# Token-major rows in the experts' feature order, and the memory's value units within the cross-attention

## The reference

```python
def memory_cross_attention(x, mem, w_q, w_kv, w_o):
    q = (x @ w_q).reshape(B, S, H, E)                  # 4 heads of 256
    kv = (mem @ w_kv).reshape(B, M, 2, H, E)
    s = jnp.einsum('bshe,bmhe->bhsm', q, kv[:, :, 0]) * (E ** -0.5)
    p = jax.nn.softmax(s, axis=-1)
    o = jnp.einsum('bhsm,bmhe->bshe', p, kv[:, :, 1])
    return o.reshape(B, S, D) @ w_o

def hier_moe(h, ...):      # top group of 4, top 2 of its 8 experts, per token
    for e in range(N_EXPERTS):
        hid = jax.nn.silu(xf @ w_gate[e]) * (xf @ w_up[e])
        y = y + combine[:, e:e + 1] * (hid @ w_down[e])
```

## Time and profile before

| | |
|---|---|
| median of 3 runs | 2835.76 us |
| the profiled execution | 2834.82 us |
| its span | 2833.0 us |
| mean granted clock | 0.972 |
| DVE busy | 1257.0 us (44%) |
| ACT busy | 1204.8 us (43%) |
| POOL busy | 981.4 us (35%) |
| HBM read | 307.22 MB |

### The profile page before, as it was taken

One profiled execution on the slowest core, in us unless ns is written; L12 is line 12 of the kernel. 1 busy time (PEld: TensorE's weight loads), 2 busy tenths in 40 slices (PEclk: granted clock), 3 DMA queues, 4 the chain that ended last, 5 costly groups with the idle time before them and its releaser, 6 DMA issues.

```text
span 2833.0 us, 36207 instructions
## 1 busy us (share of the span) xinstructions
PE 2687.5 (95%) x13862; PEld 2164.5 (76%) x13862; DVE 1257.0 (44%) x2335; ACT 1204.8 (43%) x1762; POOL 981.4 (35%) x437
## 2 busy tenths in 40 slices
PE   7998999899998999999979998999989999989998
PEld 5774886688886888888858866888858877768886
DVE  3555505443234122223256154532358336257997
ACT  3555523423234243434335324232353355346775
POOL 3221542345453333233305423444432335431000
PEclk9999999999999999999999999999998999999999
DMA  4111331233324322222113312333213422239997
GB/s 154 60 45 45 119 119 34 71 104 89 104 78 153 90 75 72 63 75 63 58 60 118 106 45 71 93 98 95 84 55 103 149 75 75 60 106 330 397 397 290
DMA packets 321050, 317.24 MB, mean 112 GB/s; under 512 B 16490, under 2 KB 278011, under 8 KB 320420
## 3 DMA queue, kind: packets, MB, share of 16 engines
q1 hardware_dynamic: 318596, 307.26, 33.4%
q0 software_dynamic: 2288, 7.88, 0.7%
q10 hardware_dynamic: 16, 0.03, 0.0%
HBM read 307.22 MB, written 19.48 MB: 115 GB/s over the span
## 4 chain that ended last, share of the span: by engine, by line
issue 48%; PE 27%; POOL 16%; DVE 3%; DMA 3%; ACT 1%; SPq 1%; POOLq 0%; ACTq 0%; DVEq 0%
POOL wl L692 12%; PE ps L2021 8%; PE ps L2022 8%; PE ps L2023 8%; POOL wl L689 4%; DMA e_raw<-in_w_up 3%; DVE e_wl L1808 2%; PE ps L2017 1%; SPq L630 1%; PE ps L2567 1%; PE ps L2332 1%; ACT e_wh L1310 0%; PE ps L2410 0%; PE ps L2429 0%; PE ps L2400 0%
## 5 line engine op out<-in xcount | busy, mean ns | idle before, releaser
L689 POOL TENSOR_TENSOR wl<-raw,wh 128x1024 fp32r<-128x1024 f32 (+1 forms) x191 | 453.1, 2372 | 1566.6 <-ACT wh L756 1566.4
L2021 PE MATMUL ps<-xh,wh 128*128 128x512 f32 x1680 | 680.9, 405 | 58.3 <-issue 29.7
L2022 PE MATMUL ps<-xh,wl 128*128 128x512 f32 x1680 | 665.6, 396 | 0.0
L2023 PE MATMUL ps<-xl,wh 128*128 128x512 f32 x1680 | 665.4, 396 | 0.0
L692 POOL TENSOR_TENSOR wl<-raw,wh 128x1024 fp32r<-128x1024 f32 (+1 forms) x191 | 478.4, 2505 | 0.0
L756 ACT ACTIVATE wh<-raw 128x1024 fp32r<-128x1024 f32 (+1 forms) x191 | 198.7, 1040 | 584.0 <-PE ps L2023 573.2
L2021 PEld LDWEIGHTS ps<-xh,wh 128*128 128x128 f32 x1680 | 322.3, 192 | 152.9 <-issue 60.3
L2023 PEld LDWEIGHTS ps<-xl,wh 128*128 128x128 f32 x1680 | 321.8, 192 | 70.4
L2022 PEld LDWEIGHTS ps<-xh,wl 128*128 128x128 f32 x1680 | 322.8, 192 | 63.5
L2021 PE MATMUL ps<-ah,wh 128*128 128x512 f32 x608 | 239.6, 394 | 5.4 <-DVE X L1534 2.4
L2023 PE MATMUL ps<-al,wh 128*128 128x512 f32 x608 | 236.7, 389 | 0.0
(11 more groups left out here) (367 smaller groups left out, 4082.3 us busy)
## 6 DMA issues: line engine op xcount, KB each, us to landing
raw<-in_ffn_w_in SPq DMA_DIRECT2D x88, 512.0 KB
raw<-in_dil_w_qkv SPq DMA_DIRECT2D x72, 512.0 KB
e_raw<-in_w_gate SPq DMA_DIRECT2D x56, 512.0 KB, 11.7
e_raw<-in_w_up SPq DMA_DIRECT2D x56, 512.0 KB, 12.9
e_raw<-in_w_down SPq DMA_DIRECT2D x56, 512.0 KB, 11.5
raw<-in_w_in SPq DMA_DIRECT2D x42, 512.0 KB
raw<-in_xatt_w_kv SPq DMA_DIRECT2D x32, 512.0 KB
raw<-in_ffn_w_out SPq DMA_DIRECT2D x32, 512.0 KB
```

The costliest lines, as they stand in the source:

```text
L689: pool.tensor_tensor(wl[:, s, 0:4, 0:n], raw[:, s, 0:4, 0:n], wh[:, s, 0:4, 0:n].bitcast(F32), ALU.subtract)
L2021: pe.matmul(dst, stat_h, mov_h, start=first, stop=False)
L2022: pe.matmul(dst, stat_l, mov_h, start=False, stop=False)
L2023: return pe.matmul(dst, stat_h, mov_l, start=False, stop=last)
```

## The change

It has two parts.

1. The four value units get numbers of their own (U_MV) behind the query units, on every engine. In the softmax stage they are placed by hand between scores and transposes. On ScalarE `values_out` waits for a value unit and makes the high part of the unit after next; VectorE's copies of the values (`cross_values`) stand between maxima and scalings. The transposes of tiles 0, 1 and 3 go to banks 2 and 3, those of tile 2 to 0 and 1. `x_q` moves to the place of `ah`, since the memory's high and low parts must last longer, and `x_e` has four buffers in place of two.
2. The step of 8 moves from TensorE's reads to ScalarE's copy into `e_tok`: it reads PSUM with the step and writes contiguously. Everything behind (`sorted_x`, `e_rows`, the product for tile 0, the transposes of later tiles) reads contiguously.

```diff
-        x_q = at("x_q", A0, [P, KC, T])
+        x_q = at("x_q", 114, [P, KC, T])
-        x_e = at("x_e", A0 + 16, [P, 2, 4 * M])
+        x_e = [at(f"x_e{n}", kb, [P, 4 * M]) for n, kb in enumerate((A0, A0 + 4, 106, 110))]
...
-        U_MQ = (24, 114)
+        U_MQ = (20, 110)
+        U_MV = (24, 114)
...
+        X_BANKS = (2, 2, 0, 2)
...
-                over(sp, U_MEM[layer], 8, lambda u, k: square(u, kv, (k * UC).v))
+                over(sp, U_MEM[layer], 4, lambda u, k: square(u, kv, (k * UC).v))
                 over(sp, U_MQ[layer], 4, lambda u, k: square(u, a["xatt_w_q"][layer], (k * UC).v))
+                over(sp, U_MV[layer], 4, lambda u, k: square(u, kv, (k * UC + D).v))
...
+                def cross_copy(i):
+                    act.wait_ge(x_tr, TT * layer + i + 1)
+                    act.activation(x_pt[:, :, i * P:(i + 1) * P],
+                                   flat[:, T * X_BANKS[i]:T * X_BANKS[i] + 1024].rearrange("p (k q) -> p k q", k=8), ACT.Copy
+                                   ).then_inc(x_ptr, 1)
+
+                def values_out(k):
+                    done(Lin(U_MV[layer] + k), 1)
+                    high(Lin(U_MV[layer] + k + 2))
+
+                for i in range(2):
+                    cross_exp(i)
+                    values_out(i)
+                cross_exp(2)
+                cross_copy(0)
+                cross_exp(3)
+                values_out(2)
+                for i in range(1, TT):
+                    cross_copy(i)
+                values_out(3)
...
-                act.activation(e_tok[:, t, :], ps[:, b:b + 2].rearrange("p b n -> p (b n)"), ACT.Copy).then_inc(r_act, 1)
+                by_rest = ps[:, b:b + 2].rearrange("p b n -> p (b n)").rearrange("p (q k) -> p k q", k=KC)
+                act.activation(e_tok[:, t, :].rearrange("p (k q) -> p k q", k=KC), by_rest, ACT.Copy).then_inc(r_act, 1)
...
+                cross_max(0)
+                cross_values(0)
+                cross_max(1)
+                cross_scale(0)
+                cross_values(1)
+                cross_max(2)
+                cross_scale(1)
+                cross_max(3)
+                cross_scale(2)
+                cross_values(2)
+                cross_scale(3)
+                cross_values(3)
...
-                for k in range(4):
-                    rows(Lin(U_MEM[layer] + 4 + k), mh, ml, tiles=2)
...
+                for i in range(2):
+                    cross_scores(i)
+                    rows(Lin(U_MV[layer] + i), mh, ml, tiles=2)
+                cross_scores(2)
+                cross_flip(0)
+                cross_scores(3)
+                rows(Lin(U_MV[layer] + 2), mh, ml, tiles=2)
+                pe.wait_ge(x_ptr, TT * layer + 1)
+                cross_flip(1)
+                emptied(pe, Lin(U_MV[layer] + 2))
+                cross_flip(2)
+                pe.wait_ge(x_ptr, TT * layer + 2)
+                cross_flip(3)
+                pe.wait_ge(x_ptr, TT * layer + 3)
+                rows(Lin(U_MV[layer] + 3), mh, ml, tiles=2)
                 pe.wait_ge(x_ptr, TT * (layer + 1))
                 for c in range(KC):
                     if c >= 4:
                         pe.wait_ge(x_al, KC * layer + c - 3)
+                    if c == 6:
+                        emptied(pe, Lin(U_MV[layer] + 3))
...
-                by_rest = e_rows[:, tile % 2, :].rearrange("p (q k) -> p k q", k=KC)
                 for c in range(4):
-                    tr = flip(ps[:, 6, c * P:(c + 1) * P], by_rest[:, 4 * half + c])
+                    k = 4 * half + c
+                    tr = flip(ps[:, 6, c * P:(c + 1) * P], e_rows[:, tile % 2, k * P:(k + 1) * P])
...
-                        feature = e_tok[:, t, :].rearrange("p (q k) -> p k q", k=KC)[:, 4 * half + c]
+                        feature = e_tok[:, t, (4 * half + c) * P:(4 * half + c + 1) * P]
```

More of the change, by code:

```diff
@@ L1048, in after_attention, with cross_exp @@
                 over(act, U_MQ[layer], 4, queries)
[L1049 to L1061, removed]
-                        act.wait_ge(x_tr, n + 1)
-                        s = 1024 * (i % 2)
-                        act.activation(x_pt[:, :, (i - 2) * P:(i - 1) * P],
-                                       flat[:, s:s + 1024].rearrange("p (k q) -> p k q", k=8), ACT.Copy
-                                       ).then_inc(x_ptr, 1)
+                def cross_exp(i):
+                    act.wait_ge(x_negm, TT * layer + i + 1)
+                    for h in range(4):
+                        at_ = 2048 + 1024 * (i % 2) + h * M
+                        act.activation(x_e[i][:, h * M:(h + 1) * M], flat[:, at_:at_ + M], ACT.Exp,
+                                       bias=negm[:, i % 2, h:h + 1], scale=1 / 16,
+                                       accum_out=sums[:, i % 2, h:h + 1]).then_inc(x_exp, 1)
@@ new lines, in cross_max @@
+                def cross_max(i):
+                    n = TT * layer + i
+                    dve.wait_ge(x_qk, n + 1)
+                    s = 2048 + 1024 * (i % 2)
+                    if n >= 2:
+                        dve.wait_ge(x_exp, 4 * (n - 1))
+                    dve.tensor_reduce(mx[:, i % 2, 0:4], flat[:, s:s + 1024].rearrange("p (h k) -> p h k", h=4),
+                                      AX_X, ALU.max).then_inc(x_max, 1)
+                    own(x_max, n + 1)
+                    dve.tensor_scalar(negm[:, i % 2, 0:4], mx[:, i % 2, 0:4], -1 / 16, None, ALU.mult
+                                      ).then_inc(x_negm, 1)
@@ new lines, in cross_scale @@
+                def cross_scale(i):
+                    n = TT * layer + i
+                    dve.wait_ge(x_exp, 4 * n + 4)
+                    dve.reciprocal(rec[:, i % 2, 0:4], sums[:, i % 2, 0:4]).then_inc(x_rec, 1)
+                    own(x_rec, n + 1)
+                    for h in range(4):
+                        dve.tensor_scalar(x_e[i][:, h * M:(h + 1) * M], x_e[i][:, h * M:(h + 1) * M],
+                                          rec[:, i % 2, h:h + 1], None, ALU.mult).then_inc(x_mix, 1)
@@ new lines, in cross_scores @@
+                def cross_scores(i):
+                    if i >= 2:
+                        pe.wait_ge(x_exp, 4 * (TT * layer + i - 1))
+                    for h in range(4):
+                        for e in range(2):
+                            mm = pe.matmul(ps[:, 4 + 2 * (i % 2) + h // 2, (h % 2) * M:(h % 2 + 1) * M],
+                                           x_q[:, 2 * h + e, i * P:(i + 1) * P], x_k[:, 2 * h + e, :],
+                                           start=e == 0, stop=e == 1)
+                    mm.then_inc(x_qk, 1)
@@ new lines, in cross_flip @@
+                def cross_flip(i):
+                    pe.wait_ge(x_mix, 4 * (TT * layer + i) + 4)
+                    for k in range(8):
+                        tr = flip(ps[:, X_BANKS[i] + k // 4, (k % 4) * P:(k % 4 + 1) * P], x_e[i][:, k * P:(k + 1) * P])
+                    tr.then_inc(x_tr, 1)
+                for i in range(2):
[3 more added lines that the diff above has]
+                cross_flip(0)
```

54 lines of the change are left out of this document (5 added, 49 removed).

## The result

The changed kernel takes 2828.91 us (median of 20 runs, 2826.07 to 2835.55) against 2834.69 us for the kernel before in its 20 runs beside them. The ratio is 0.9985, with a 95% interval of 0.9978 to 0.9992: about 4.3 us faster (the medians stand 5.8 us apart), where the forecast was 13.4. The time lies at the upper end of the range.

A forecast was written before the change was run, and what follows sets the result against it. TensorE was taken as busy 95% of the span, the experts as bound by the weights' transfer. Cross-attention -13.9, clock +1.7, experts -1.2 gave -13.4 us: 2822.3 against the median 2835.76; range 2814 to 2830.

The forecast's parts named there:

- within that gap: Softmax stage: VectorE's scaling of tile 3 ends at 38.4, inside the one new gap of 1.3 us before transposes 3.
- Values leave, the queries follow; wait of 1.35 us: Cross-attention behind the keys: 24.16 us of values leave, query unit 0 waits 1.35 us for bank 1; query end -22.8 us.
- The clock at query unit 0: Start of the query stage: TensorE's clock may fall to half; one fall in two layers, +1.7 us, range 0 to +5.8.
- rival 1: Query unit 0: low clock in both layers, and longer, +5.8 us in place of +1.7, 2826 us; chance 0.14.
- Rival 5: Query stage: the clock stays down through it; one whole stage at half pace gives 2864 us; slower, chance 0.04.
- The softmax stage, 59.8 us: Last query matmul to first output matmul, with values inserted: 59.8 us against 43.8 before, growing by 16.0 in layer 0.
- Rival 3: Softmax stage: a late copy or low half grows the gap to 4 us, clock falls in the product; 2833.4 us; chance 0.10.
- Rival 4: Routing: ScalarE's strided PSUM reads are slow, +1 us, and the transfer's dip isn't filled, +1.2; 2824.5 us; chance 0.05.
- 48 transposes, -1.7 us: Later expert tiles: transposes with a contiguous operand save 0.035 us each of 0.15, together 1.7 us.
- The experts, "I take 1.2 us" less: Routing and experts: of 8 us saved in the 64 passes, 1.2 us reaches the end; bounds 0 and 8.
- what can be won is the dip: Weights' transfer when SyncE begins issuing again: three us of low DMA rate, 484 KB short, worth 1.2 us.
- Rival 2: Experts: they pass on the whole 8 us saved in the 64 passes; 2815.5 us; chance 0.12.

The follow-up runs named there:

- key_copy_first: The changed kernel, but ScalarE copies bank 1 of the last key unit before it makes the next unit's high part; ratio 0.9967 to the kernel before.

## Why the prediction was right or wrong, point by point

The mechanism came as foretold in the main: the units moved, and the product ran at full clock. Of the 13.4 us only 4.3 came, since the falls of the clock were counted too few, since one scaling was placed "within that gap" and wasn't, and since the experts lost where they were to win.

- *Values leave, the queries follow; wait of 1.35 us:* right, 1.15.
- *The clock at query unit 0, "one fall in two layers: +1.7":* mis-sized. Over twelve stages it cost 1.4 us per layer, so 2.7; in the profiled execution 2.9 + 1.4 = 4.3, near rival 1 (5.8). In key_copy_first, with the second wait taken out, it fell in neither layer. Rival 5, the clock down through the query stage, is out: no stage lost more than 3.4 us of low clock before the scores.
- *The softmax stage, 59.8 us:* the replay was right but for one step, "the scaling of tile 3 waits for values 2 and ends at 38.4, within that gap". It ran against GpSimd's low half, and the gap was 2.2, not 1.3: +0.9 per layer. I had the low halves only as something to be waited for. Once the scaling is moved, the gap is 1.34 us and the stage takes the replayed time.
- *The clock in the softmax stage:* the sum had one fall, at the scores. In the ten stages with the gap of 2.2 us there was one fall, at the scores or behind the gap, in five (57.6 to 57.7 us from scores to output unit), and both in the other five (59.3 to 59.4): half a fall of 1.7 us, 0.85 per layer, more than the sum. Rival 3 had this form, the gap grown and the clock falling behind it, though for other reasons and at a higher price.
- *The product at full clock, 13.4 us:* right, 13.33.
- *64 passes in 7.4 us; ScalarE's strided reads free:* right, 7.3 us and 1026 ns. Rival 4 is out. *48 transposes, -1.7 us:* wrong, they don't get shorter. The 0.15 us each was the busy time of groups of four, in which the whole duration of the last one counts; from start to start they took 0.109 us before the change already. (The changed kernel's mean of 281 ns for 273 is a low stretch of the clock among them; seven of the kernels with contiguous reads have 272 to 274.)
- *The experts, "I take 1.2 us" less:* wrong in sign. The last weights' copy came 1.1 us later: 263.0 behind the mark on average of the seven executions with short passes and the orders of SyncE and GpSimd unchanged, 261.9 of the three without (0.8 at unit 58). That the transfer is the bound, and the 8 us are absorbed, held. The failed step is "what can be won is the dip": I looked at who waits for the passes, not at who runs beside what the passes had held back. Rival 2 is out. For this step and for the scaling of tile 3, the rule on the shared ports that is named above bears on the change, and I hadn't weighed it.
- *Sum:* 1.0 (query clock) + 3.0 (gap and clock in the softmax stage) + 2.3 (experts) = 6.3 of the 9.1 us between 13.4 and 4.3. The 3.0 is read from the ten stages, 58.5 us on average from scores to output unit where the replay has 57.05; the two terms above, added up, would give 3.5. Another 0.7 is in what was compared: the one execution that the replay starts from was that much longer in its two stages than the average of the four stages with the old cross-attention. The rest, 2.1 us, no longer stands out from the ratio's interval, 2 us to either side.

What stays open is a part outside the change. The dilated attention, from its first to its last transpose, took 469.3 and 469.4 us in the two kernels with the old cross-attention, and 469.4 to 476.6 in the eleven with the new one, mostly 470.5; in the changed kernel's profiled execution 474.5, which is why this one is so slow. TensorE waits much in its last 50 us (14 to 17 us), and the granted clock differs there from execution to execution: low clock cost 5.1 us of this stretch in the two, and 5.1 to 15.4 in the eleven, the most where it took longest. No run tells whether the earlier end of layer 0 brings this about.

## What to carry to other kernels

Where TensorE waits for a copy, look at what the copying engine does just before it: here high parts of 2.1 us each stood ahead of copies of 0.4 to 1.0 us, and exchanging them was worth 0.6 to 0.8% where moving whole units had brought 0.15%. Price a wait with the clock that it may cost, which in these traces was nothing or 1.7, 3.4 or 5.1 us in the cross-attention. And of a step that gets faster, ask which engines start sooner and what they then run beside, VectorE and GpSimd above all.

## What the runs showed of the hardware

- A low stretch of TensorE's clock cost about 1.7, 3.4 or 5.1 us in the stage. Whether it came was not the same in two layers of one execution: behind the wait of 2.75 us at the scores in 14 of 18 stages, behind the gap of 2.2 in 8 of 10, behind 1.34 in none of two, behind 0.78 in none of eight.
- VectorE's scaling (SBUF to SBUF) waited for the end of a GpSimd instruction, 3.23 us for 1.14; and a GpSimd scatter that started within VectorE's weight split ended 0.82 to 0.84 us behind it, so took 1.9 to 2.9 us for 0.95.
- ScalarE reads PSUM with a step of 32 bytes as fast as contiguously: 1026 ns for 128 x 1024 float32. TensorE's stationary operand with that step costs in the 64 passes, 15.4 us against 7.3 (one weight load 0.33 us against 0.19). In the 48 transposes the same step costs nothing: 0.109 us from start to start with it and without, though a weight load takes 0.19 us with it and 0.14 without.
